# Eight modulation pieces of layer 1 computed in layer 1's state-space scan instead of layer 0's latent stage and attention

## What is computed

```python
for layer in range(DEPTH):
    need_ctx = layer < DEPTH - 1
    mod_l = (jax.nn.silu(c) @ ada_w[layer] + ada_b[layer]).reshape(bsz, N_MOD, 1, d)
    mod_c = (jax.nn.silu(c_ctx) @ ada_w[layer] + ada_b[layer]).reshape(N_MOD, d)
    h_lat = modulate(x_lat, norm1_g[layer], mod_l[:, 0], mod_l[:, 1])
    h_ctx = modulate(x_ctx, norm1_g[layer], mod_c[0], mod_c[1])
    ...
    x_lat = x_lat + mod_l[:, 2] * y_lat
    h2_lat = modulate(x_lat, norm2_g[layer], mod_l[:, 3], mod_l[:, 4]).reshape(bsz * n_lat, d)
    ...
    x_lat = x_lat + mod_l[:, 5] * f_lat.reshape(bsz, n_lat, d)
```

## Time and profile before

| | us |
|---|---|
| median of 3 runs | 1630.97 |
| lowest, highest | 1630.47, 1633.42 |
| span of the profiled execution | 1626.5 |
| latent stage, in the span | 155.7 to 247.7 |
| attention of layer 0 | 247.7 to 362.0 |
| projections and scan of layer 1 | 900.9 to 1054.0, the scan's loop from 1011 |

### The profile page before, as it was taken

One profiled execution on the slowest core, in us unless ns is written; L12 is line 12 of the kernel. 1 busy time (PEld: TensorE's weight loads), 2 busy tenths in 40 slices (PEclk: granted clock), 3 DMA queues, 4 the chain that ended last, 5 costly groups with the idle time before them and its releaser, 6 DMA issues. The chain is left out here.

```text
span 1626.5 us, 34895 instructions
## 1 busy us (share of the span) xinstructions
PE 1223.2 (75%) x14230; PEld 709.2 (44%) x14231; DVE 538.9 (33%) x1487; ACT 405.4 (25%) x932; POOL 39.3 (2%) x83
## 2 busy tenths in 40 slices
PE   4898878985999997687652998788678765655652
PEld 3355655543556554344321647444345432322321
DVE  1538555337222221121114365873412111101102
ACT  1254224213222322122113123552122211111100
POOL 0201101000000000000001000000000000000000
PEclk8999989997999998898886899989699877777776
DMA  8611988349899999999996400083899999999995
GB/s 314 233 63 36 371 325 306 137 161 376 347 417 428 430 428 429 430 428 429 430 427 237 135 32 1 16 347 147 333 416 428 429 429 428 429 429 429 429 428 204
DMA packets 84160, 515.12 MB, mean 317 GB/s; under 512 B 13917, under 2 KB 18242, under 8 KB 58746
## 3 DMA queue, kind: packets, MB, share of 16 engines
q1 hardware_dynamic: 74664, 489.60, 73.4%
q10 hardware_dynamic: 5730, 13.81, 2.2%
q0 software_dynamic: 3696, 10.73, 1.7%
HBM read 497.10 MB, written 17.01 MB: 316 GB/s over the span
## 5 line engine op out<-in xcount | busy, mean ns | idle before, releaser
L1578 PE MATMUL bank<-sb_ring,sb_scratch 128*32 128x256 f32 x3904 | 271.5, 440 | 154.1 <-DMA sb_ring<-in_moe_w_up 142.4
L1578 PEld LDWEIGHTS bank<-sb_ring,sb_scratch 128*32 128x32 f32 x3904 | 141.6, 126 | 281.6 <-issue 224.2
L1659 DVE TENSOR_TENSOR sb_scratch<-sb_scratch,bank 128x128 f32<-128x128 f32 x88 | 25.3, 288 | 701.2 <-ACT sb_scratch L1612 701.2
L1616 ACT ACTIVATE sb_scratch<-bank 32x256 f32<-32x256 f32 x352 | 132.1, 375 | 274.2 <-PE bank L1588 271.1
L1578 PE MATMUL bank<-sb_scratch 128*32 128x256 f32 x1728 | 117.9, 433 | 59.9 <-DMA sb_scratch<-in_moe_w_up 56.1
L1558 PE MATMUL bank<-sb_h,sb_scratch 128*32 128x256 f32 x2256 | 140.9, 384 | 6.1 <-DVE sb_scratch L1646 6.1
L1612 ACT ACTIVATE sb_scratch<-bank 128x128 f32<-128x128 f32 x88 | 24.4, 278 | 423.9 <-PE bank L1578 423.8
L1588 PE MATMUL bank<-sb_ring,sb_scratch 128*32 128x256 f32 x1856 | 111.5, 380 | 8.7 <-issue 8.2
L1578 PEld LDWEIGHTS bank<-sb_scratch 128*32 128x32 f32 x1728 | 62.4, 124 | 114.1 <-issue 89.9
L1558 PEld LDWEIGHTS bank<-sb_h,sb_scratch 128*32 128x32 f32 x2256 | 74.3, 111 | 55.2 <-DVE sb_scratch L1646 6.6
L1588 PEld LDWEIGHTS bank<-sb_ring,sb_scratch 128*32 128x32 f32 x1856 | 62.6, 110 | 51.5 <-issue 19.8
(11 more groups left out here) (365 smaller groups left out, 1371.9 us busy)
## 6 DMA issues: line engine op xcount, KB each, us to landing
sb_ring<-in_moe_w_gate SPq DMA_DIRECT2D x44, 2048.0 KB, 27.0
sb_ring<-in_moe_w_up SPq DMA_DIRECT2D x44, 2048.0 KB, 31.7
sb_ring<-in_moe_w_down SPq DMA_DIRECT2D x41, 2048.0 KB, 34.8
sb_ring<-in_ada_w SPq DMA_DIRECT2D x21, 2048.0 KB, 16.1
sb_scratch<-in_moe_w_gate SPq DMA_DIRECT2D x20, 2048.0 KB, 30.5
sb_scratch<-in_moe_w_up SPq DMA_DIRECT2D x20, 2048.0 KB, 33.9
sb_scratch<-in_moe_w_down SPq DMA_DIRECT2D x20, 2048.0 KB, 36.2
sorted_out<-sb_scratch ACTq DMA_DIRECT2D x88, 128.0 KB, 6.1
```

Of the source, the lines that this page charges most:

```text
L1578: last = nc.tensor.matmul(c.bank(1, 2, FQ)[MB * q:MB * q + MB, :, :], m.xt[:, k, :], m.gu[j][:, :, k, q * FQ:(q + 1) * FQ], start=k == 0, ...
L1616: last = nc.scalar.activation(m.yb[j][:, q * DQ:(q + 1) * DQ], c.ps[3][MB * q:MB * q + MB, 0:DQ], ACT.Copy)
L1659: v.tensor_tensor(m.hm, m.sg, c.ps[1][:, FQ:2 * FQ], ALU.mult).then_inc(hm_ready, 1)
```

## The change

The group `late` keeps 12 pieces (8 of layer 0, the first 4 of layer 1), so its share a unit is 12/8. The group `last` has 8 pieces, (1, 4) to (1, 11): the mixer's gate and the three vectors of the experts. It leaves attention of layer 0, with its loads, products, finishes, tables and store, and goes to `project_ssd_stage`. There its ring has two slots (ring 1, behind the last two projection chunks), its tables lie in the context half of x, and its products use banks 0 and 5 in turn. Expert 0's weights are now loaded right behind `ab_w_out`. Nothing is computed less or more in sum: 24 pieces stay 24.

```diff
-def attention_stage(..., sp_work=None, sp_end=None, md=None, out=None):
+def attention_stage(..., sp_work=None, out=None):
...
-                if j in ada_after:
-                    a = ada_after[j]
-                    if out_after and j > min(out_after):
-                        pe.wait_ge(out_added, len([b for b in out_after if b < j]))
...
-                    md.product(a, 7).then_inc(ada_product, 1)
...
-def project_ssd_stage(c, m, w_in, used):
+def project_ssd_stage(c, m, md, w_in, used):
...
+    def ada_bank(a):
+        return 5 * (a % 2)
...
             sp.wait_ge(side, SMALL)
+            for a in range(md.n):
+                if a < R:
+                    sp.wait_ge(product, (GATE, GATE + 4)[a])
+                else:
+                    sp.wait_ge(ada_product, a - R + 1)
+                md.load_weights(sp, a, ada_in[a % R])
+            sp.wait_ge(ada_done, md.n)
+            md.store(sp, stored)
+            sp.wait_ge(stored, 16 * md.Q * len(md.segments))
...
+            md.preset_tables(preset)
+            pool.wait_ge(preset, 2)
+            md.load_tables(pool, tables_in)
+            pool.wait_ge(tables_in, 16 * md.n_loads)
             nc.clear_and_free_semaphores(used)
...
                 for n in (2 * w + 4, 2 * w + 5):
                     if n < NS:
                         row(n)
+                if w == 0:
+                    pe.wait_ge(columns, 1)
+                if w >= 2:
+                    pe.wait_ge(ada_done, w - 1)
+                pe.wait_ge(ada_in[w % R], 16 * (w // R + 1))
+                md.product(w, ada_bank(w)).then_inc(ada_product, 1)
                 pair_product(w)
             pe.wait_ge(consts, 2)
+            pe.wait_ge(ada_done, md.n)
...
+            md.spread_columns(columns)
+            dve.wait_ge(tables_in, 16 * md.n_loads)
             for n in range(4):
                 exponent(n)
             for w in range(NS // 2):
...
+                if w:
+                    dve.wait_ge(ada_product, w)
+                    md.finish(w - 1, ada_bank(w - 1), ada_done)
                 if w in (3, 5, 7):
                     finish((w - 3) // 2)
             finish(3)
+            dve.wait_ge(ada_product, md.n)
+            md.finish(md.n - 1, ada_bank(md.n - 1), ada_done)
...
-        late = Modulation(c, [(0, 4, Modulation.CH), (1, 0, 6)], ...
+        late = Modulation(c, [(0, 4, Modulation.CH), (1, 0, 4)], ...
...
-        last = Modulation(c, [(1, 6, Modulation.CH)], [(c.ring[0], j * KC * BANK) for j in range(3)],
-                          c.ring[1][:, 8192:9216], c.ring[1][:, 9216:10240])
+        last = Modulation(c, [(1, 4, Modulation.CH)], [(c.ring[1], j * KC * BANK) for j in range(2)],
+                          c.x_flat[:, 2 * D:2 * D + 1280], c.x_flat[:, 2 * D + 1280:2 * D + 1536])
...
         def loads(sp):
             sp.dma_start(m.wo, ins["ab_w_out"].rearrange("o (k p) n -> p (o k) n", p=P)).then_inc(wo_in, 16)
+            load_expert(c, mo, sp, 0, 0)
```

More of the change, by code:

```diff
@@ L878, in _, with attention_stage @@
                     md.finish(a, 2 + a % 2, ada_done)
-def attention_stage(c, units, qt, kt, v_of, scale, dst_t, p, pt, width, sink=None, mask=None, sp_work=None, sp_end=None, md=None, out=None):
+def attention_stage(c, units, qt, kt, v_of, scale, dst_t, p, pt, width, sink=None, mask=None, sp_work=None, out=None):
     nc = c.nc
@@ L891, in attention_stage @@
     den_r = c.sem("sink_exp")
-    ada_after = {}
-    if md:
-        ada_after = dict(zip((3, 4, 5, 8, 9, 12), range(md.n)))
-        ada_in = [c.sem(f"ada_w_in{j}") for j in range(len(md.ring))]
-        ada_product, ada_done, stored, preset, tables_in, columns = (
-            c.sem(x) for x in ("ada_product", "ada_row_done", "mod_stored", "mod_tables_preset", "mod_tables_in", "cond_columns"))
     nm, rs, es = ([c.stat[:, a + s:a + s + 1] for s in range(4)] for a in (0, 4, 8))
@@ L910, in _ @@
                 out.load_gates(sp)
-            if md:
-                for a in range(len(md.ring)):
-                    if a == 1:
-                        sp.wait_ge(tables_in, 16 * md.n_loads)
-                    md.load_weights(sp, a, ada_in[a])
             if sp_work:
                 sp_work(sp)
-            if md:
-                R = len(md.ring)
-                for a in range(R, md.n):
-                    sp.wait_ge(ada_product, a - R + 1)
-                    md.load_weights(sp, a, ada_in[a % R])
-                sp.wait_ge(ada_done, md.n)
-                md.store(sp, stored)
-                if sp_end:
-                    sp_end(sp)
-                sp.wait_ge(stored, 16 * md.Q * len(md.segments))
-        @block.gpsimd
-        def _(pool):
-            if md:
-                md.preset_tables(preset)
-                pool.wait_ge(preset, 2)
-                md.load_tables(pool, tables_in)
         @block.tensor
@@ L975, in _ @@
                         pe.wait_ge(out_added, u)
-                    if md:
-                        pe.wait_ge(ada_done, len([b for b in ada_after if b < j]))
                     out.product(u, 7).then_inc(out_product, 1)
-                if j in ada_after:
-                    a = ada_after[j]
-                    if out_after and j > min(out_after):
-                        pe.wait_ge(out_added, len([b for b in out_after if b < j]))
-                    if a == 0:
-                        pe.wait_ge(columns, 1)
-                    else:
-                        pe.wait_ge(ada_done, a)
-                    pe.wait_ge(ada_in[a % len(md.ring)], 16 * (a // len(md.ring) + 1))
-                    md.product(a, 7).then_inc(ada_product, 1)
                 turn(2 * j)
@@ L1050, in _ @@
             maximum(1)
-            if md:
-                md.spread_columns(columns)
             for u in range(n):
@@ L1913, in project_ssd_stage @@
         S(x) for x in ("head_mean", "head_root", "head_ready", "head_turned", "head_t_copied", "queries_copied"))
+    R = len(md.ring)
+    ada_in = [S(f"ada_w_in{j}") for j in range(R)]
+    ada_product, ada_done, stored, preset, tables_in, columns = (
+        S(x) for x in ("ada_product", "ada_row_done", "mod_stored", "mod_tables_preset", "mod_tables_in", "cond_columns"))
+    def ada_bank(a):
+        return 5 * (a % 2)
     ss_k, ss_q = c.stat[:, 16:16 + NT * KVH], c.stat[:, 16 + NT * KVH:16 + NT * KVH + LT * NH]
@@ L2328, in program @@
         attention_stage(c, units, m.qt, lambda h: m.kt[:, h, :], lambda h, k: m.v[:, k, h * VD:(h + 1) * VD],
-                        QK ** -0.5, m.attn_t, m.p, m.pt, QK, sp_work=loads, sp_end=lambda sp: load_expert(c, mo, sp, 0, 0), md=last, out=out)
+                        QK ** -0.5, m.attn_t, m.p, m.pt, QK, sp_work=loads, out=out)
         def first_weights(sp):
@@ L2345, in program @@
         m = MixerCD(c)
-        project_ssd_stage(c, m, w_in, c.done_semaphores([*w_in, *mo.semaphores]))
+        project_ssd_stage(c, m, last, w_in, c.done_semaphores([*w_in, *mo.semaphores]))
         wo_in = c.sem("cd_wo_in")
```

7 lines of the change are left out of this document (1 added, 6 removed).

## The result

| | before | after |
|---|---|---|
| median of 6 runs each, us | 1630.72 | 1640.26 |
| lowest, highest | 1629.28, 1633.82 | 1634.99, 1650.07 |
| span of the profiled execution | 1626.5 | 1633.2 |
| latent stage | 92.0 | 81.7 |
| attention of layer 0 | 114.3 | 108.0 |

The ratio is 1.0046, 95% interval 1.0024 to 1.0068: the changed kernel is slower by about half a per cent, where 0.3% faster was forecast. In the spans the difference is +6.7 us: -10.3, -6.3, +21.4 and +2.5 in the four stages of the table, and -0.7 in all others together.

The account below looks back on a forecast made before the run. Loads were taken to bound the latent stage, TensorE and its waits attention of layer 0; the scan had TensorE continuous mid-loop and DMA idle. -12.2 - 7.6 + 14.6 = -5.2 us, from 1630.97 to 1625.8; 8 in 10: 1622.2 to 1630.6.

Parts of the forecast that it names:

- Latent stage: Loads end this stage; 14 pieces become 12, last piece 10.6 us earlier, last product 1.7 us quicker: -12.2 us.
- the fourth rival: Latent stage: the queue runs dry once as load 11 goes out late; 3 us lost, time 1629; chance 0.06.
- Attention of layer 0: Six pieces leave; shorter pairs, no wait for `ab_w_out`, column spreading off VectorE's path: -7.6 us, bounds -5.1 and -8.6.
- The scan: Layer 1's scan: eight pieces arrive, last pair product 14.1 us later, tail 0.5: +14.6 us, bounds 11.8 and 19.4.
- just in time: Scan: loads 2 to 5 land 8.3 us after issue, 0.7 to 0.9 before their products are due.
- The formula of the prediction: Scan, loads setting the pace: with load time L, the last pair product moves by 3 x L - 12.3 us.
- the point where the sign turns: Third rival, two slots too few in the scan: gain gone from 10.6 us a load; at 16.2, 1648 us; chance 0.05.
- all old waits filled: Scan's lower bound: no wait for a load, old VectorE waits take in work: 15.7 - 3.9 = 11.8 us.
- the tail: Behind the scan's loop, mean products wait for all finishes and start together with the last square: +0.5 us.
- The second rival: Scan iterations 6 and 7: TensorE falls to 1.2 GHz in new waits; term 18 to 19.4, time about 1630.0; chance 0.12.
- The range: Whole kernel: 8 in 10 for 1622.2 to 1630.6 us, within summed bounds of -10.5 to +3.8 us.
- the late queue: Latent stage's queue running dry once because load 11 goes out late: 3 us of the 12.2 lost; chance 0.06.

Follow-up runs that it names:

- the repeat: The changed kernel again, nothing edited, for a second profile and its spread: 1637.39 us, ratio 1.0036 to the kernel before.
- filling: Small identity matmuls, result unread, in TensorE's waits in both attention stages, against the changed kernel: 1635.12 us, ratio 1.0016 to the kernel before; also added to other kernels.

## Why the prediction was wrong

**Latent stage: forecast -12.2, measured -10.3.** The mechanism held, the last product at the full clock too. What came on top is the fourth rival in small: the queue ran thin once (266 for 363 GB/s), behind a clock of 0.66 ahead of the second unit's products. The last product came 1.8 us late, not 3. In the repeat the clock was 1.00 there, the rate 350 GB/s and the stage 80.5 us, which fits; no run tests it alone. The prediction took TensorE's pace in the middle of this stage from the one execution it had. That execution also had the shortest stage of its kind: with 14 pieces it took 92.0, 94.4, 94.8 and 95.1 us in four profiles, with 12 pieces 80.5 to 83.2 in ten, so the forecast of -12.2 was nearer to the truth than this one difference.

**Attention of layer 0: forecast -7.6, measured -6.3.** The full-width pairs 3 to 5 came out at 4.55 us (4.54 forecast), pair 9 at 3.09, and pairs 8 and 12 saved 0.4 each where 0.5 was given. The last output product took 8.80 us for 7.11, a fall of the clock worth 1.7; without it the term is -8.0. The runs above showed what the prediction missed here. From 50 to 105 us after the start of the stage the granted clock was 1.00 in all five profiles with the pieces, and 0.97, 0.97, 1.00, 1.00, 0.88 and 0.97 in the six that had neither pieces nor filling. So the pieces seem to have kept the clock up as well; the profiles agree with it, but no run tests it alone.

**The scan: forecast +14.6, measured +21.4. This is the step that failed**, and in it the sentence "each lands 8.3 us later, 0.7 to 0.9 before its product is due: just in time". The row was that of a load with no other beside it. In the loop a product comes every 5.5 us and a load takes at least 8.3, so two are always under way for part of the time, and they share the engines: 9.8 to 12.0 us. What would have told so was at hand: pieces landed 5.41 and 5.21 us apart at the full rate, so two loads that overlap entirely take nearly 11 us each (an estimate, twice 5.41), and a need for one every 5.5 us is a need for nearly all of the rate. The formula of the prediction does hold: pieces 3, 5 and 7 took 12.0, 9.8 and 10.9 us, and 3 x L with their mean of 10.9, less 12.3, gives +20.4; the last pair product moved by 20.9. The prediction had also named the point where the sign turns, 10.6 us a load, and gave that case 0.05 with 16.2 us for the load, while by the rows just named a value near the point was the one to expect. With the loads taken out of the loop the stage lost 10 us of the 21.4, and with a third slot 9.6, all loads kept: the two runs that show the cause.

By terms: 11.2 for products without waits (11.8 forecast with all old waits filled), 8.2 of waits for weights (3.1 forecast), 1.6 of a low clock in iteration 6 (2.66 and 2.65 us for 1.95 and 1.73): 21.0 of 21.4. From the last pair product to the stage's end it is 9.5 us for 8.9, the 0.5 that the tail was given; it is contained in the 11.2.

**The clock in the scan.** The second rival expected 1.2 GHz in iterations 6 and 7. It came in one of them. The Trainium skill's rule ("TensorE: Matmul & The Clock Gate", section "HAM oscillation — how this bites in real kernels", bursts with a wait for a load between them fall back each time) was right for one of five waits: behind 1.39, 1.70, 0.97 and 1.86 us the products took 1.95 to 1.96, behind 2.29 us 2.66. The length of the wait does not decide it alone: in the scan of the changed kernel with small matmuls in its waits a product took 1.96 us behind a wait of 2.89, and one 2.95 behind 2.38.

**Attention of layer 1: not in the sum, +2.5.** I do not count this to the change. The stage varied from 50.4 to 59.5 us with unchanged code, 53.0 and 57.5 in two profiles of the changed kernel itself, and the profile of before happened to be the shortest of these. Whether the change makes the falls more frequent there is open: kernels that kept all pieces where they were had 56.5 and 57.2 us too, but with small matmuls in or ahead of the stage.

**The range** ended at 1630.6. Its upper end took 19.4 for the scan, from loads of 9.2 us, and there it was 2 us short. In the spans the late queue, attention of layer 0 and attention of layer 1 added 1.9, 1.3 and 2.5. The medians differ by 9.5 us, more than the spans, since the profiled execution after lies 5.3 us below its median and that of before 2.4.

## What to carry to other kernels

A load's time from a row where it runs alone is a lower bound. Before relying on it, divide the bytes by the full rate and compare with the period at which loads are wanted; where the two are near, count each load at the time of all those under way together, or give the ring one slot more. And price a moved piece of work at both places: the two pieces at the end of a stage bound by loads were worth about 5 us each there and cost 1.2 each in the scan, while the six that already stood in waits cost more at the new place than they had at the old. And before a stage's length is compared across two profiles, see how much it varies where nothing was changed: 3.7 us from the start of the last projections to the first product in the scan, and 9 in attention of layer 1.

## What the hardware showed

- Loads of 2 MB from issue to landing: 8.3 to 8.7 us alone, 9.8 to 12.0 with one other under way for a part of the time, 13.4 when asked for 0.6 us behind another.
- The same wait of 1.20 us in the same code left TensorE at 2.4 GHz in one execution and put it at 1.2 in another, pair after pair (5.4 or 6.9 us a pair). The Trainium skill tells of such a pattern in "TensorE: Matmul & The Clock Gate", section "A second HAM failure mode: psum-queue depth-cycling": frequent short idle times between groups of matmuls make the clock go to and fro. The traces agree.
- Matmuls of no use in those waits held the clock: over the last 26 us of attention of layer 1 it was 1.00 in all five profiles with them, and without them 0.80 to 0.87 in eight of nine (1.00 in that of before). Eight of them, placed while the clock was low, took 3.62 us for 1.95.
- Work taken off TensorE in attention of layer 0 left waits in which the clock could fall: 112.3 us for the stage in one profile, 106.3 to 109.6 in five others, 107.7 to 107.8 in three with filling.
